# Two blocks of columns in turn at the start of four phases, and the places between phases worked in halves

## The reference

```
h = rms_norm(x, g_mix); mixed = three kinds of attention on h @ w_in; x += mixed @ w_out
x += memory_cross_attention(rms_norm(x), rms_norm(mem))
h = rms_norm(x, g_ffn); g, u = split(h @ w_up)
x = x + (silu(conv3(g) + b) * u) @ w_down; x = rms_norm(x, g_final)
# second block
x += 0.5 * rms_norm((silu(h1 @ w_gate) * (h1 @ w_up)) @ w_down)      # ff1, h1 = rms_norm(x)
x += rms_norm(attention_out @ w_out + recurrence_out @ w_out)        # nsa attention and a gated recurrence
x += 0.5 * rms_norm((silu(h3 @ w_gate) * (h3 @ w_up)) @ w_down)      # ff2
x += rms_norm(sigmoid(h4 @ w_ple_gate) * (p @ w_ple_proj))           # ple
```

## Time and profile before

| | us |
|---|---|
| median of 3 runs (lowest, highest) | 3412.84 (3411.91, 3415.19) |
| the profiled execution, its own time | 3412.71 |
| its span | 3410.4 |
| TensorE busy | 3243.6 (95%) |
| VectorE busy | 2116.0 (62%) |
| ScalarE busy | 1575.9 (46%) |
| GpSimd busy | 89.3 (3%) |

### The profile page before, as it was taken

How to read it: one execution, slowest core, us unless ns; L and a number is a source line. 1 busy time by engine, 2 the same in 40 slices (tenths; PEclk the granted TensorE clock), 3 DMA queues, 4 the chain that set the end, 5 groups by cost and what they waited for, 6 DMA issues and landing times.

```text
span 3410.4 us, 51789 instructions
## 1 busy us (share of the span) xinstructions
PE 3243.6 (95%) x19800; PEld 2879.7 (84%) x19800; DVE 2116.0 (62%) x2266; ACT 1575.9 (46%) x1873; POOL 89.3 (3%) x38
## 2 busy tenths in 40 slices
PE   8999999999999997999999998998979999999976
PEld 7989987888888886888888887988968888888865
DVE  5666666666665547555655458655875555554476
ACT  5444455555544334444444344445544444443343
POOL 0000200000000000000000000000100000000001
PEclk9999999999999998999999998999989999999988
DMA  7545554666666664666666664743446665655533
GB/s 248 177 145 150 183 173 144 191 188 186 190 189 187 191 186 135 191 193 189 188 187 189 188 190 138 217 116 105 161 136 187 189 185 184 195 187 191 187 127 103
DMA packets 321856, 595.63 MB, mean 175 GB/s; under 512 B 18276, under 2 KB 41988, under 8 KB 321732
## 3 DMA queue, kind: packets, MB, share of 16 engines
q1 hardware_dynamic: 313856, 587.27, 56.0%
q10 hardware_dynamic: 7876, 6.63, 0.6%
HBM read 591.70 MB, written 2.13 MB: 174 GB/s over the span
## 4 chain that ended last, share of the span: by engine, by line
PE 90%; DVE 5%; ACT 2%; issue 1%; DMA 0%; POOL 0%; POOLq 0%; ACTq 0%; DVEq 0%
PE acc L541 26%; PE acc L543 24%; PE acc L546 23%; PE acc L579 4%; PE acc L582 4%; PE acc L581 4%; ACT wh L989 1%; DVE wl L1419 1%; DVE T L1538 1%; DVE X L1543 0%; ACT OPR L1040 0%; DVE SM L1913 0%; ACT HF L1264 0%; ACT S L1264 0%; DVE RSTD L1497 0%
## 5 line engine op out<-in xcount | busy, mean ns | idle before, releaser
L1419 DVE TENSOR_TENSOR wl<-raw,wh 128x1024 fp32r<-128x1024 f32 x1112 | 1388.4, 1257 | 1114.2 <-ACT wh L989 1112.6
L989 ACT ACTIVATE wh<-raw 128x1024 fp32r<-128x1024 f32 x1112 | 1165.8, 1057 | 1365.2 <-PE acc L546 1084.0
L543 PEld LDWEIGHTS acc<-OPR,wl 128*128 128x128 f32 x4992 | 946.2, 190 | 208.2
L541 PE MATMUL acc<-OPR,wh 128*128 128x512 f32 x2658 | 1049.7, 400 | 46.1 <-DVE OPR L1521 40.4
L543 PE MATMUL acc<-OPR,wl 128*128 128x256 f32 x4992 | 1015.6, 280 | 0.0
L546 PE MATMUL acc<-OPR,wh 128*128 128x512 f32 x2334 | 926.2, 397 | 0.0
L541 PEld LDWEIGHTS acc<-OPR,wh 128*128 128x128 f32 x2658 | 509.9, 192 | 69.8 <-issue 35.5
L543 PEld LDWEIGHTS acc<-HR,wl 128*128 128x128 f32 x2208 | 414.8, 188 | 94.9
L541 PE MATMUL acc<-HR,wh 128*128 128x512 f32 x1138 | 447.0, 396 | 3.5 <-DVE T L1433 2.3
L543 PE MATMUL acc<-HR,wl 128*128 128x256 f32 x2208 | 439.6, 278 | 0.0
L546 PEld LDWEIGHTS acc<-OPR,wh 128*128 128x128 f32 x2334 | 439.4, 188 | 0.0
(11 more groups left out here) (312 smaller groups left out, 1929.9 us busy)
## 6 DMA issues: line engine op xcount, KB each, us to landing
raw<-in_w_up SPq DMA_DIRECT2D x176, 512.0 KB, 4.4
raw<-in_ff_w_gate SPq DMA_DIRECT2D x176, 512.0 KB, 3.7
raw<-in_ff_w_up SPq DMA_DIRECT2D x176, 512.0 KB, 4.4
raw<-in_ff_w_down SPq DMA_DIRECT2D x176, 512.0 KB, 3.8
raw<-in_w_in SPq DMA_DIRECT2D x170, 512.0 KB, 4.1
raw<-in_w_down SPq DMA_DIRECT2D x88, 512.0 KB, 3.7
raw<-in_w_out SPq DMA_DIRECT2D x64, 512.0 KB, 3.7
raw<-in_w_ple_gate SPq DMA_DIRECT2D x32, 512.0 KB, 3.7
```

Of the source, the lines that this page charges most:

```text
L541: pe.matmul(acc[:, b + t, :], wh[:, s, col:col + P], x, start=first, stop=False)
L543: mm = pe.matmul(acc[:, b + t, 0:T], wl[:, s, col:col + P], x[:, 0, :], start=False, stop=last and t % 2 == 0)
L989: act.activation(wh[:, s, :], raw[:, s, :], ACT.Copy).then_inc(hi_done, 1)
L1419: dve.tensor_tensor(wl[:, s, :], raw[:, s, :], wh[:, s, :].bitcast(F32), ALU.subtract)\
```

## The change

Four phases, `up`, `ff1_up`, `ff2_up` and `ple_gate`, are now called PAIRED. Their first two blocks are done unit by unit in turn: unit 0 of block 0, unit 0 of block 1, unit 1 of block 0, and so on, and the loads come in this order. The splits of units 4 to 15 stand in pairs behind slices 5, 7, ..., 15; the two blocks are collected together (`take_pair`, `collect_pair`), and the late statistic comes in the third block after its unit 1. The added squares and their fold now stand behind the last slice. In the up phases the second pair of blocks is written out too.

At the five seams the last block is taken and collected in two halves of two tiles. The first three quarters are folded earlier (`early_fold`: two units before the last split in the down phases, at unit 13 in wo_r, ahead of the last block's collection in ple_proj). ScalarE squares each half of the last quarter, and TensorE sums these squares itself, with four further products into the same bank (`post_stat`). ScalarE's last split stands behind these squares. The first four slices of the new x are formed one by one. The rest is bookkeeping (semaphores, counts, the bank of the statistic).

The diff, cut to its core:

```diff
+PAIRED = ["up", "ff1_up", "ff2_up", "ple_gate"]
...
+                def first_pair():
+                    for u in range(2 * ph["upc"]):
+                        src = weight(u % 2)[u // 2 * rows:(u // 2 + 1) * rows, bass.ds(col(u % 2, 0), width)]
+                        load(ph["u0"] + u, 0, src.rearrange("(k p) n -> p k n", p=P))
                 def block(c, i):
...
+            def post_stat(name):
+                pe.wait_ge(colsum_ready, N[name] + 1)
+                pe.wait_ge(acc_free, PH[UNDER[name]]["c0"] + 3)
+                pe.matmul(acc[:, post_bank(name), 0:T], ones[:, :], colsum, start=True, stop=False)
+                for h in range(2):
+                    pe.wait_ge(post_sq, 2 * POSTS[name] + h + 1)
+                    for k in range(2):
+                        at = 512 * h + T * k
+                        mm = pe.matmul(acc[:, post_bank(name), 0:T], ones[:, :], S[:, at:at + T],
+                                       start=False, stop=h == 1 and k == 1)
+                mm.then_inc(stat_ready, 1)
+                pe.wait_ge(var_ready, N[name] + 1)
...
-                pe.wait_ge(acc_free, ph["c0"] + 1)
+                pe.wait_ge(acc_free, ph["c0"] + (2 if ph["name"] in PAIRED else 1))
...
+                    for v in range(2 * ph["upc"] if paired else ph["upc"]):
+                        b = bank_of(g + v % 2) if paired else bank_of(g)
+                        u = v // 2 if paired else v
+                        n = ph["u0"] + c * ph["upc"] + v
...
+            def take_pair(ph, norm):
+                u0 = ph["u0"]
+                split(u0 + 16, 0)
+                split(u0 + 17, 0)
+                take(ph, 0, 0, used=u0 + 15)
+                split(u0 + 18, 0)
+                take(ph, 1, 0)
+                split(u0 + 19, 0)
+                split(u0 + 20, 0)
+                std(norm, bank=stat_bank(ph))
+            def take_halves(ph, name):
+                g = ph["c0"] + 3
+                b = bank_of(g)
+                act.wait_ge(units_used, ph["u0"] + 4 * ph["upc"])
+                act.wait_ge(acc_free, g)
+                act.activation(T1[:, 0:2, :], acc[:, b:b + 2, T:2 * T], ACT.Copy).then_inc(half_t1, 1)
+                act.activation(T1[:, 2:4, :], acc[:, b + 2:b + 4, T:2 * T], ACT.Copy).then_inc(t1_full, 1)
+            def post_squares(name):
+                src, done, count = last_quarter(name)
+                act.wait_ge(colsum_ready, N[name] + 1)
+                for h in range(2):
+                    if h == 0:
+                        act.wait_ge(half_y, POSTS[name] + 1)
+                    else:
+                        act.wait_ge(done, count)
+                    act.activation(S[:, 512 * h:512 * (h + 1)], src[:, 2 * h:2 * h + 2, :].rearrange("p c t -> p (c t)"),
+                                   ACT.Square).then_inc(post_sq, 1)
...
+                    if post and c == 3:
+                        splits(ph, c, i, 0, ph["upc"] - 1)
+                        take_halves(ph, post)
+                        post_squares(post)
+                        splits(ph, c, i, ph["upc"] - 1)
...
+                    elif norm in FIRST_X and c < 3:
+                        act.wait_ge(first_x, 3 * FIRST_X[norm] + c + 1)
+                    elif norm in SRC and (c % 4 == 0 or c == 3 and norm in FIRST_X):
                         act.wait_ge(ssq_src, SRC[norm] + c // 4 + 1)
                     act.activation(dst(c), src(c), ACT.Copy, scale=v(gain, c)).then_inc(xs_hi, 1)
+                    if paired and c >= 5 and c % 2 == 1:
+                        split(ph["u0"] + c - 1, 0)
+                        split(ph["u0"] + c, 0)
...
+                def first_pair():
+                    take_pair(ph, norm)
+                    split(ph["u0"] + 21, 0)
+                    silu(0, 0, T2, 11 * f + 1, lambda: None)
+                    split(ph["u0"] + 22, 0)
+                    high(0, 0, 11 * f + 1)
...
+            post_squares("mix_post")
+            split(ph["u0"] + 15 + LEAD, 0)
...
+            def collect_half(ph, name, h, dst, done):
+                g = ph["c0"] + 3
+                b = bank_of(g) + 2 * h
+                if h == 0:
+                    dve.wait_ge(half_t1, HALF_T1[name])
+                else:
+                    dve.wait_ge(t1_full, t1_count(g))
+                dve.tensor_tensor(dst, acc[:, b:b + 2, 0:T], T1[:, 2 * h:2 * h + 2, :], ALU.add).then_inc(done, 1)
+            def early_fold(name):
+                dve.wait_ge(ssq_done, POOLED[name] + 1)
+                chain(dve.tensor_tensor(S[:, 2048:2560], S[:, 0:512], S[:, 512:1024], ALU.add))
+                dve.tensor_tensor(S[:, 1024:1280], S[:, 2048:2304], S[:, 2304:2560], ALU.add)\
+                   .then_inc(colsum_ready, 1)
...
+                        if post and c == 3:
+                            last = ph["upc"] - 1
+                            splits(ph, c, i, 0, max(last - 2, 0))
+                            early_fold(post)
+                            splits(ph, c, i, max(last - 2, 0), last)
+                            evac(ph, c, i, halves=post)
+                            splits(ph, c, i, last)
...
+            def collect_pair(ph, norm, dst):
+                u0 = ph["u0"]
+                split(u0 + 16, 0)
+                split(u0 + 17, 0)
+                collect(ph, 0, 0, dst[0])
+                split(u0 + 18, 0)
+                collect(ph, 1, 0, dst[1])
+                split(u0 + 19, 0)
+                split(u0 + 20, 0)
+                collected(ph, 1, 0)
+                rstd(norm)
...
+                        for h in range(2):
+                            t = T2[:, 2 * h:2 * h + 2, :]
+                            if h == 0:
+                                collect_half(ph, halves, h, t, half_c)
+                                dve.wait_ge(half_c, 1)
+                            else:
+                                collect_half(ph, halves, h, t, acc_free)
+                                collected(ph, c, i)
+                            x = X[:, 12 + 2 * h:14 + 2 * h, :]
+                            dve.tensor_tensor(x, x, t, ALU.add).then_inc(ssq_src if h else half_y, 1)
...
+                    if update and c == 0:
+                        update(0, 0)
+                    if update and c < 3:
+                        update(0, c + 1)
+                    elif update and c % 4 == 0:
                         update(c // 4)
                     dve.wait_ge(xs_hi, first + c + 1)
                     dve.scalar_tensor_tensor(dst[:, c, 1, :], src(c), v(gain, c), dst[:, c, 0, :].bitcast(F32),
                                              ALU.mult, ALU.subtract).then_inc(xs_lo, 1)
-                if ph:
+                    if paired and c >= 5 and c % 2 == 1:
+                        split(ph["u0"] + c - 1, 0)
+                        split(ph["u0"] + c, 0)
+                if paired:
+                    for g in (1, 2, 3):
+                        add_square(sq, g)
+                    fold(sq)
...
+                    if one is not None:
+                        t, x = T2[:, one, :], X[:, one, :]
+                        chain(dve.scalar_tensor_tensor(t, y[:, first + one, :], v(gain, one), RSTD[:, :],
+                                                       ALU.mult, ALU.mult))
+                        dve.tensor_tensor(x, x, t, ALU.add).then_inc(done if one == 3 else first_x, 1)
+                        return
...
+                def first_pair():
+                    n = 11 * f + 1
+                    collect_pair(ph, norm, [T2[:, :, :], G[:, :, :]])
+                    dve.tensor_tensor(T2[:, :, :], T2[:, :, :], bc(RSTD[:, :], 4), ALU.mult).then_inc(g_pre, 1)
+                    split(ph["u0"] + 21, 0)
+                    if conv:
+                        taps(0, 0, T2, n, lambda: None)
+                    dve.wait_ge(g_silu, n)
+                    chain(dve.tensor_tensor(T2[:, :, :], SIL[:, :, :], bc(RSTD[:, :], 4), ALU.mult))
+                    dve.tensor_tensor(T2[:, :, :], T2[:, :, :], G[:, :, :], ALU.mult).then_inc(u_mul, 1)
+                    split(ph["u0"] + 22, 0)
+                    low(0, 0, n)
...
+                if n == 13:
+                    early_fold("mix_post")
...
```

More of the change, by code:

```diff
@@ L327, in program @@
                ("ff1", 16), ("mixp", 16), ("nsa", 16), ("ff2", 16), ("ple", 16), ("p", 1)]
+        FIRST_X = {n: i for i, n in enumerate(["ff1_pre", "mix_pre", "ff2_pre", "ple_pre"])}
+        POSTS = {n: i for i, n in enumerate(["final", "ff1_post", "mix_post", "ff2_post", "ple_post"])}
+        UNDER = {"final": "down", "ff1_post": "ff1_down", "mix_post": "wo_r", "ff2_post": "ff2_down", "ple_post": "ple_proj"}
+        HALF_T1 = {n: i + 1 for i, n in enumerate(["final", "ff1_post", "ff2_post", "ple_post"])}
         SRC = {n: 4 * i for i, n in enumerate(["ffn", "final", "ff1_pre", "mix_pre", "ff2_pre",
@@ L520, in gemm @@
                 chunks = 1024 // width
+                late = 2 if name in PAIRED else 1
                 def block(c, i):
```

(32 more changed lines are left out.)

253 lines of the change are left out of this document (152 added, 101 removed).

## The result

Four executions of the changed kernel took 3379.14 us in the median (3376.84 to 3381.03), four of the kernel before 3412.38 (3409.15 to 3415.19): a ratio of 0.990, 95% interval 0.9886 to 0.9914. The profiled execution took 3376.84 us, its span 3374.6.

A forecast was written before the change was run, and what follows sets the result against it. TensorE, holding 90% of the chain of waits, bounds the kernel, so time is won only where it stands still. Won 32.4 less lost 6.25 is 26.2 us net, from 3412.71 to 3386.5 us, range 3380 to 3400.

The forecast's parts named there:

- part 1: Four seams: collecting and squaring the last block in halves brings the square root earlier, 13.25 us won together.
- part 2: Behind the seams: forming the first slices one by one starts the next phase earlier, 2.4 us won, none in in_c.
- part 3: Paired phases: two blocks in turn remove 9.65 us of slice waits and 7.1 us of late-statistic idle and half clock.
- (a): Third block of paired phases: unit 16 needs block 0 collected, 1.0 us lost, 0.2 in ff2_up and 0.8 in ple_gate.
- (b): In `up`: the convolution's chain delays split 22, so TensorE waits for unit 22, 2.0 us lost, bounds 0 to 3.5.
- (c): Tail after ple_proj: the early fold now stands ahead of the block's collection, 3.25 us lost, bounds 2.5 and 4.4.
- All good is -5: Whole kernel: if all the unknowns go well, the time is 5 us under the forecast.
- R5: More is won: split 22 in `up` comes in time and the tail takes its lower bound, 3382.5 us, chance 0.08.
- R1: Seams: a pause behind the table load, a second load or half-clock sums cost time, 3390 to 3395 us, chance 0.12.
- R2: Paired phases feed badly: VectorE's hand-overs or third-block collections leave 10 to 16 us unwon, about 3400 us, chance 0.10.
- R3: Seams: halves bring nothing, split and table load arrive as late as before, 13.25 us gone, 3400 us, chance 0.05.
- R4: Paired phases: a ring of waits over some 3 us brings half clock; seven such waits give 3427 us, chance 0.05.

The follow-up runs named there:

- e1: Changed kernel with whole collections, fold and statistic of before in all five places, pairs and single first slices kept; 3386.58 us, ratio 0.9931 to the kernel before.
- e6: Changed kernel with the first four slices behind a seam updated and scaled as a group again; 3382.71 us, ratio 0.9913 to the kernel before.
- e2: Changed kernel with ple_gate alone back to one block after the other, the other three phases in pairs; 3389.07 us, ratio 0.9933 to the kernel before.
- e9: Changed kernel with unit 22's split in `up` moved into existing waits and unit 23's in its old place; 3376.00 us, ratio 0.9898 to the kernel before.
- e4: Changed kernel with the tail alone as before, ple_proj's last block collected whole, fold behind it; 3375.83 us, ratio 0.9892 to the kernel before.
- a0_after: The changed kernel again, unedited, as base of the variants, beside the kernel before; 3378.11 us, ratio 0.9901.
- e5: Changed kernel with the early fold of ple_post behind the two halves instead of ahead of them; 3378.10 us, ratio 0.9896 to the kernel before.
- e7: Changed kernel with the last split ahead of the halves again in down, ff1_down and ff2_down; 3383.41 us, ratio 0.9912 to the kernel before.
- e10: Changed kernel with unused products of ones by ones on TensorE in the pauses of the four seams; 3369.00 us, ratio 0.9887 to the kernel before.
- e12: Changed kernel with the edits of e9, e4 and e10 together; 3368.78 us, ratio 0.9881 to the kernel before.

## Why the prediction was off by 6.4 us

The direction and each mechanism came as forecast; sizes were off, all but one to the same side. Won in the seams' and phases' stretches: 16.8 (seams) + 2.5 (ff1) + 5.7 (ff2) + 9.9 (ple), less 0.9 (up, down) and 1.3 (tail), is 32.6 against 26.2. The median itself lies 7.4 us under the forecast of 3386.5; the last 1.0 is within what executions of one kernel differ by.

| step | forecast | measured | from |
|---|---|---|---|
| part 1, halves in four seams | +13.25 | +13.1 | e1 |
| part 2, first slices | +2.4 | +3.65 | e6 |
| part 3, ff1: wait, statistic | +2.4 | +2.5 | table |
| part 3 and (a), ff2 | +4.6 | +5.7 | table |
| part 3 and (a), ple | +8.75 | +9.9 | table; e2: 9.1 |
| (b) `up` | -2.0 | -0.9 | table; e9 |
| (c) tail | -3.25 | -1.3 to -1.4 | table; e1, e4 |

**(c), the tail, is the term furthest off (1.9).** It and the next three steps together made the time fall under the range. The chain from GpSimd's end to the root was right (6.91 us measured, 7.1 forecast). The failed step is that I kept GpSimd's end where it was: the earlier trace rows showed it, 9.9 us after ple_proj's last product, with VectorE working beside it. The early fold holds VectorE still there, and GpSimd ends 8.1 after it. e4 puts VectorE's work back and the 1.75 with it.

**"Idle falls to the 0.45 that `up` shows"** failed next: it fell to nothing, in four phases, 1.8 us in all. 0.45 of the 1.1 missed in (b) is this; the wait itself was sized well (2.0; 1.77 came). Why the statistic waits 0.55 to 1.1 us in in_c and not at all behind a pair was not tried.

**"In in_c ... 0"** in part 2 failed by 0.95: the start that was won is not lost again as a longer wait (e6). The gain per seam with post_norm is 0.95 and not 0.75 (e6), and in seam 1 0.8, not 0.9.

**(a)**, the third block, was to cost 0.2 and 0.8; it costs nothing and 0.17. Some 0.4 us of ff2 stay unexplained by waits (1.20, 2.83 and 1.22 are gone, 5.7 were won), in a stretch that varies by 0.8.

**The seams.** Seams 2 and 4 came within 0.12 us of the forecast place of the root, seam 1 at E+6.40 (6.7). In seam 3 the half clock took 0.6 of its gain. I had counted TensorE's products as fitting "since a pause of 2.83 left the clock up": that held for the pause of 1.70 and not for 2.37 and 2.50, where the eight passes mostly took 3.34 us or a little more, 2.40 in some executions. It was one case, and the trace of the kernel before held the opposite one. The 8 us behind its wait of 2.85 us in in_c (at 2081.63), then behind the 2.83 of the earlier trace rows:
```profile
2081.60:2089.60 8.00, 7.97 (x39) 0.79 0.45 131
2524.90:2532.90 8.00, 8.00 (x45) 1.00 0.50 136
```
The same wait in in_c was followed by 0.79 in the changed profile and by 1.00 in a0_after. After pauses of this length the clock falls in one execution and not in the next, with the same kernel.

**The bounds.** "All good is -5" and R5's 3382.5 are not what their terms give: split 22 in time is worth 2.0 and the tail's lower bound 0.75, together 2.75, which is 3383.8. No term for the first slices in in_c or for a statistic without idle was in them, and these came.

**The rivals.** R1: one load per seam, no pause behind it, no load ahead of the squares; out. Its half-clock sums came in part, in seams 1 and 3, and cost seam 3 its 0.6. R2: out by e2. R3: out by e1. R4: no ring of waits in the paired phases; out. R5 named the right side, with half a reason: the tail was cheap, but not by its lower bound, and split 22 did not come in time.

## What to carry over

Read each effect in its own stretch of the trace: stretches that no edit touches varied by 6 us here, while seams 2 and 4 repeat within 0.02. Before moving work away from an engine, look at which others share the time: a stretch measured beside VectorE's work is not what GpSimd takes without it. And where TensorE must pause, the pause costs its own length and can cost some us at half clock behind it. Work without a result in the pause bought 9.1 us by the medians in one kernel and 4.7 in another; it doesn't hold the clock each time, and where TensorE waits for slices right behind the pause, a full clock brought nothing.

## What the runs showed of the hardware

- GpSimd's 128x1024 square took 1.89 us beside an idle VectorE, 2.23 and 2.76 beside a working one, its addition 2.34, 2.67 and 3.20; it works both ways. VectorE's half multiplication of 0.69 us took 1.99 in e5:
```profile
3349.37 1.99 DVE L2331 TENSOR_TENSOR HF<-T,HF 128x512 f32<-128x512 f32 x1
```
- The granted clock after a pause: behind 1.70 us eight passes took 1.99 or 2.00 in every profile, behind 3.36 us 3.78 in both seams of e7. Behind pauses of 2.82 to 2.85 us the next 8 us had 1.00 in some places and executions and 0.79 or 0.63 in others. With products of ones in it, a seam left the next 4 us at full clock in four of eight cases (e10 and e12); without them every seam of every profile, the kernel before included, is followed by 0.50 to 0.65.
- The same instructions up to the first product of `up` took from 543.1 to 548.9 us.
